# Expert loop of a hybrid layer: one-hot stationary gather with transposes, combining gates by transposes, gate and up biases on two row groups

## The reference, cut to what matters

```python
def swiglu_expert(xb, wg, bg, wu, bu, wd, bd):
    gate = jnp.minimum(xb @ wg + bg, SWIGLU_LIMIT)
    up = jnp.clip(xb @ wu + bu, -SWIGLU_LIMIT, SWIGLU_LIMIT)
    glu = gate * jax.nn.sigmoid(SWIGLU_ALPHA * gate)
    return ((up + 1.0) * glu) @ wd + bd

# routed_moe: logits = hf @ wr + br; top_v, top_i = lax.top_k(logits, 4)
# gates = jax.nn.softmax(top_v); the output of a token is the sum over its
# four experts of gate * swiglu_expert(token)
```

## Time and profile before

| | |
|---|---|
| time, median of three runs | 1285.4 us (1281.82 to 1287.41) |
| span of the profiled execution | 1284.3 us |
| TensorE busy | 1223.1 us, 95% of the span |
| VectorE, ScalarE, GpSimd busy | 250.6, 183.5, 19.8 us |
| L1431, weight products, 3072 records | 456.1 + 226.8 us |
| L1415, gather, 1056 records | 128.5 us |
| L1424, biases, 256 records | 69.6 us |
| L1406, spread, 66 records | 37.0 us |
| moved by DMA | 455.34 MB, 355 GB/s over the span |

### The profile page before, as it was taken

The page is one execution under the profiler, slowest core; times in us unless marked ns, Lnnn a source line. Parts: engine busy times, 40 slices in busy tenths (PEclk is TensorE's granted clock), DMA queues, the critical chain, the costliest instruction groups (busy, mean ns, idle before and its releaser), DMA issues.

```text
span 1284.3 us, 15147 instructions
## 1 busy us (share of the span) xinstructions
PE 1223.1 (95%) x6020; PEld 552.0 (43%) x6020; DVE 250.6 (20%) x535; ACT 183.5 (14%) x305; POOL 19.8 (2%) x40
## 2 busy tenths in 40 slices
PE   6699999999999999999999999999999999999995
PEld 1388965543333334443333333333333333333332
DVE  1334571511111111111111111111111111111113
ACT  1122431201111111111111111111111111111111
POOL 3000000000000000000000000000000000000000
PEclk9599999969999999999999999999999999999998
DMA  9994359529999999999999999999999999999971
GB/s 316 333 331 140 118 202 360 197 110 373 398 407 406 406 407 405 403 409 408 405 407 406 405 408 403 405 404 410 405 404 408 407 406 406 407 408 406 405 303 33
DMA packets 135160, 455.34 MB, mean 355 GB/s; under 512 B 7967, under 2 KB 21299, under 8 KB 135014
## 3 DMA queue, kind: packets, MB, share of 16 engines
q1 hardware_dynamic: 132080, 446.73, 89.3%
q0 software_dynamic: 2064, 6.98, 1.6%
q10 hardware_dynamic: 998, 1.37, 0.4%
HBM read 453.35 MB, written 1.70 MB: 354 GB/s over the span
## 4 chain that ended last, share of the span: by engine, by line
PE 82%; ACT 3%; DVE 1%; issue 0%
PE bank L1431 53%; PE bank L1415 10%; PE bank L1424 5%; PE bank L1441 5%; PE bank L1406 3%; PE bank L1307 2%; ACT k_pool L623 1%; PE bank L1102 1%; ACT at_pool L615 1%; PE bank L1134 1%; PE bank L1109 1%; PE bank L1463 0%; PE bank L1375 0%; PE bank L1343 0%; DVE xres L1063 0%; DVE k_pool L1062 0%
## 5 line engine op out<-in xcount | busy, mean ns | idle before, releaser
L1431 PE MATMUL bank<-ring,at_pool 128*64 128x512 f32 x2048 | 456.1, 598 | 0.0
L1431 PEld LDWEIGHTS bank<-ring,at_pool 128*64 128x64 f32 x2048 | 141.9, 137 | 310.5 <-issue 310.5
L1431 PE MATMUL bank<-ring,k_pool 128*64 128x512 f32 x1024 | 226.8, 595 | 23.0 <-ACT k_pool L623 23.0
L1431 PEld LDWEIGHTS bank<-ring,k_pool 128*64 128x64 f32 x1024 | 70.7, 137 | 158.5 <-issue 127.9
L1415 PEld LDWEIGHTS bank<-keyT,rows 128*128 128x128 f32 x1056 | 123.7, 196 | 28.6 <-issue 28.6
L1005 DVE TENSOR_SCALAR k_pool<-bank 128x512 f32<-128x512 f32 x32 | 22.1, 692 | 578.9 <-PE bank L1431 578.9
L1415 PE MATMUL bank<-keyT,rows 128*128 128x64 f32 x1056 | 128.5, 281 | 0.0
L615 ACT COPY at_pool<-bank 128x512 f32<-128x512 f32 x33 | 19.3, 586 | 443.3 <-PE bank L1415 443.3
L1424 PE MATMUL bank<-kv_pool,cumT 32*64 32x512 f32 x256 | 69.6, 620 | 0.0
L1009 DVE TENSOR_SCALAR k_pool<-bank 128x512 f32<-128x512 f32 x32 | 22.1, 692 | 226.9 <-PE bank L1431 226.9
L1441 PE MATMUL bank<-d_pool,at_pool 64*128 64x512 f32 x264 | 65.6, 615 | 0.7 <-ACT d_pool L625 0.7
(11 more groups left out here) (300 smaller groups left out, 590.5 us busy)
## 6 DMA issues: line engine op xcount, KB each, us to landing
ring<-in_w_gate SPq DMA_DIRECT2D x128, 1024.0 KB, 9.5
ring<-in_w_up SPq DMA_DIRECT2D x128, 1024.0 KB, 8.7
ring<-in_w_down SPq DMA_DIRECT2D x128, 1024.0 KB, 7.4
ring<-in_w_mod SPq DMA_DIRECT2D x24, 1024.0 KB, 10.1
ring<-in_w_in SPq DMA_DIRECT2D x13, 1024.0 KB, 12.5
ring<-in_w_out SPq DMA_DIRECT2D x4, 1024.0 KB, 6.7
k_pool<-in_const_masks POOLq DMA_DIRECT2D x1, 1024.0 KB, 8.0
g<-in_b_mod POOLq DMA_DIRECT2D x2, 512.0 KB, 12.3
```

The costliest lines, as they stand in the source:

```text
L1431: ins = mm(bank[CAP * half:CAP * (half + 1), :], lhsT(2 * r + kk), w[:, kk, 512 * half:512 * (half + 1)], start=m == 2 and r == 0 and kk = ...
```

## The change

- The gather takes the one-hot matrix `Ptok` (128x64) as the stationary operand and 512 columns of `rows` as the moving one: four matmuls into bank 3, which then holds the tokens in rows, its two halves of columns on the two halves of the partitions. ScalarE copies them to `xg`, four transposes bring them into bank 1 (`tokens_transpose`), ScalarE copies that to `xe`.
- The gates: VectorE makes `Gtok`, tokens x slots (twice over, 128 columns) with the gate in place of the one, and two transposes give its transpose in bank 0; `slot_gates` is one copy. `spread`, and the transposes and copy of the ranks ahead of the loop, are gone.
- The biases of gate and up lie on partitions 0 to 31 and 32 to 63, `pick` has 64 rows, and the four bias matmuls of both stand together ahead of the gate product (`biases`).
- The order on TensorE is now: biases, gate product, combine, up product, gather, gate transposes, transposes of the activations, token transposes, down product. VectorE does `up_step` ahead of `slot_gates`. ScalarE does sigmoid, copy to `xg`, copy to `aT`, copy to `xe`, copy to `ysb`.
- The identity of the expert numbers comes with the constants and no longer from GpSimd. One `keep_clock` matmul ahead of the loop is gone.

The core of the diff:

```diff
+        bias_gu = moe_pool[0:2 * NE, 0:D]
+        bias_d = moe_pool[0:NE, D:2 * D]
+        xg = moe_pool[:, 2 * D:2 * D + 512]
+        Gtok = moe_pool[:, 2 * D + 512:2 * D + 768].rearrange("p (t s) -> p t s", t=2)
...
             with act.Fori(0, NE) as e:
                 sigmoid_step(e)
+                gathered_out(e + 1)
+                activations_out(e)
                 tokens_out(e + 1)
-                down_steps(e)
+                down_out(e)
...
+                slots = cst[:, C_SLOTROW:C_SLOTROW + P]
                 for t in range(2):
...
+                    r = rank[:, t, bass.ds(e, 1)] if off is None else rank_off[:, t:t + 1]
+                    V.tensor_scalar(Ptok[:, t, :], slots[:, 0:CAP], r, None, ALU.is_equal)
+                    ins = V.tensor_scalar(Gtok[:, t, :], slots, r, gate[:, t, bass.ds(e, 1)], ALU.is_equal, ALU.mult)
                 ins.then_inc(ev("route_ready"), 1)
...
+            def slot_gates(count, buf, bank=B[0]):
+                dve.wait_ge(ev("gT_ps"), count + 1)
+                V.tensor_copy(gT[:, buf, :], bank[:, 256:512]).then_inc(ev("gT_ready"), 1)
...
                     gate_step(e)
-                    dve.wait_ge(ev("xe_ps"), e + 1)
+                    dve.wait_ge(ev("gT_ps"), e + 1)
                     route(e + 1, 1 - u)
+                    up_step(e)
                     slot_gates(e + 1, 1 - u)
-                    up_step(e)
...
+            def gather(count):
                 pe.wait_ge(ev("route_ready"), count + 1)
-                mm(B[3], pick[:, buf, :], rgT, start=True, stop=True).then_inc(ev("bc_ps"), 1)
+                pe.wait_ge(ev("xg_sb"), count)
+                for t in range(2):
+                    for half in range(2):
+                        ins = mm(B[3][CAP * half:CAP * (half + 1), :], Ptok[:, t, :], rows[:, t, 512 * half:512 * (half + 1)],
+                                 start=t == 0, stop=t == 1)
+                ins.then_inc(ev("xg_ps"), 1)
+            def gates_transpose(count, emptied, bank=B[0]):
+                pe.wait_ge(ev("gate_min"), emptied)
+                pe.wait_ge(ev("gT_ready"), count)
+                for t in range(2):
+                    ins = tr(bank[:, 256 + P * t:256 + P * (t + 1)], Gtok[:, t, :], ident)
+                ins.then_inc(ev("gT_ps"), 1)
+            def tokens_transpose(count):
+                pe.wait_ge(ev("xg_sb"), count + 1)
+                pe.wait_ge(ev("xe_ready"), count)
+                for q in range(4):
+                    ins = tr(B[1][:, P * q:P * (q + 1)], xg[:, P * q:P * (q + 1)], ident)
+                ins.then_inc(ev("xe_ps"), 1)
+            def biases(buf, count):
                 pe.wait_ge(ev("gT_ready"), count + 1)
+                pe.wait_ge(ev("xe_ready"), count + 1)
+                for m in range(2):
+                    r = slice(NE * m, NE * (m + 1))
+                    for half in range(2):
+                        mm(B[m][CAP * half:CAP * (half + 1), :], pick[r, buf, :], bias_gu[r, 512 * half:512 * (half + 1)],
+                           start=True, stop=False)
...
             open_sums(0)
-            gather(0, between=lambda: open_sums(1))
-            keep_clock(1, B[2])
+            pe.wait_ge(ev("gT_ready"), 1)
+            tokens_transpose(0)
+            open_sums(1)
...
                     e = i * 2 + u
-                    pe.wait_ge(ev("xe_ready"), e + 1)
-                    product(B[0], 0, u, xe_tile, e)
+                    biases(u, e)
+                    product(B[0], 0, xe_tile, e)
                     combine(1 - u, e + 1)
-                    spread(1 - u, e + 1)
-                    product(B[1], 1, u, xe_tile, e)
+                    product(B[1], 1, xe_tile, e)
                     gather(e + 1)
-                    down(u, e)
+                    gates_transpose(e + 1, e + 1)
+                    activations_transpose(e)
+                    tokens_transpose(e + 1)
+                    down(e)
```

More of the change, by code:

```diff
@@ L442, in _ @@
             pool.wait_ge(ev("cat_ps"), 4)
[L443 to L444 removed]
+            small_load("mbias_loaded", bias_gu[0:NE, :], b_gate[0])
+            small_load("mbias_loaded", bias_gu[NE:2 * NE, :], b_up[0])
+            small_load("mbias_loaded", bias_d, b_down[0])
             pool.wait_ge(ev("mbias_loaded"), 48)
@@ L609, in _, with gathered_out @@
             act.wait_ge(ev("rgT_ps"), 1)
-            nc.scalar.copy(rgT, B[1][0:NE, :]).then_inc(ev("rgT_ready"), 1)
+            nc.scalar.copy(gateT, B[1][0:NE, 0:2 * P]).then_inc(ev("gateT_ready"), 1)
+            def gathered_out(count):
+                act.wait_ge(ev("xg_ps"), count + 1)
+                nc.scalar.copy(xg, B[3]).then_inc(ev("xg_sb"), 1)
             def tokens_out(count):
                 act.wait_ge(ev("xe_ps"), count + 1)
-                nc.scalar.copy(xe.rearrange("p k s -> p (k s)"), B[3]).then_inc(ev("xe_ready"), 1)
+                nc.scalar.copy(xe.rearrange("p c s -> p (c s)"), B[1]).then_inc(ev("xe_ready"), 1)
             def sigmoid_step(count):
@@ L1394, in _ @@
             for t in range(2):
-                tr(B[1][0:NE, P * t:P * (t + 1)], rank[:, t, 0:NE], ident)
-                ins = tr(B[1][0:NE, 256 + P * t:256 + P * (t + 1)], gate[:, t, :], ident)
+                ins = tr(B[1][0:NE, P * t:P * (t + 1)], gate[:, t, 0:NE], ident)
             ins.then_inc(ev("rgT_ps"), 1)
             mm(B[0][:, 64:65], cst[:, C_STRI:C_STRI + P], flag, start=True, stop=True).then_inc(ev("pos_ps"), 1)
-            def spread(buf, count):
+            def gather(count):
@@ L1405, in spread @@
                 pe.wait_ge(ev("route_ready"), count + 1)
-                mm(B[3], pick[:, buf, :], rgT, start=True, stop=True).then_inc(ev("bc_ps"), 1)
-            def gather(count, between=None):
-                pe.wait_ge(ev("gT_ready"), count + 1)
[L1411 to L1424, removed]
+                pe.wait_ge(ev("xg_sb"), count)
[3 more added lines that the diff above has]
+                                 start=t == 0, stop=t == 1)
@@ new lines, in biases, with product @@
+            def biases(buf, count):
+                pe.wait_ge(ev("gT_ready"), count + 1)
+                pe.wait_ge(ev("xe_ready"), count + 1)
[4 more added lines that the diff above has]
+                           start=True, stop=False)
+            def product(bank, m, lhsT, count):
@@ L1444, in xe_tile, with activations_transpose @@
             def xe_tile(k):
-                return xe[:, k, :]
+                return xe[:, k % 4, CAP * (k // 4):CAP * (k // 4 + 1)]
             def a_tile(k):
                 return aT[:, k % 4, CAP * (k // 4):CAP * (k // 4 + 1)]
-            def down(buf, count):
+            def activations_transpose(count):
                 pe.wait_ge(ev("a_ready"), count + 1)
@@ L1455, in down @@
                 ins.then_inc(ev("aT_ps"), 1)
+            def down(count):
                 pe.wait_ge(ev("aT_ready"), count + 1)
-                product(B[2], 2, buf, a_tile, count)
+                product(B[2], 2, a_tile, count)
             def open_sums(t):
                 for half in range(2):
-                    mm(B[4 + 2 * t + half], rgT[:, 256 + P * t:256 + P * (t + 1)], mbias[:, 2, 512 * half:512 * (half + 1)],
+                    mm(B[4 + 2 * t + half], gateT[:, P * t:P * (t + 1)], bias_d[:, 512 * half:512 * (half + 1)],
                        start=True, stop=False)
             keep_clock(2, B[2])
-            pe.wait_ge(ev("rgT_ready"), 1)
-            spread(0, 0)
+            gather(0)
+            pe.wait_ge(ev("gateT_ready"), 1)
+            gates_transpose(0, 0, B[1])
             pe.wait_ge(ev("onehot_ready"), 1)
@@ L1495, in _ @@
                     with pe.If(n_over > j):
-                        spread(0, j + (NE + 1))
                         gather(j + (NE + 1))
[L1498 to L1501, removed]
+                        gates_transpose(j + (NE + 1), j + NE)
+                        tokens_transpose(j + (NE + 1))
+                        biases(0, j + (NE + 1))
+                        product(B[0], 0, xe_tile, j + NE)
+                        product(B[1], 1, xe_tile, j + NE)
+                        activations_transpose(j + NE)
+                        down(j + NE)
                         combine(0, j + (NE + 2))
```

69 lines of the change are left out of this document (30 added, 39 removed).

## The result

Over four runs each, the changed kernel takes 1245.6 us (1242.4 to 1249.6), the one before 1283.6 (1281.3 to 1287.4): a ratio of 0.970, interval 0.967 to 0.972. The profiled execution has a span of 1241.7 us and a time of 1243.5. The forecast was 1241 of time and 1239.8 of span.

The account below looks back on a forecast made before the run. TensorE set the pace (30.97 us per expert), loads close behind (30.6); after the change the loads set the end. First issue 270, loads 951.3, tail 1.8 and 16.7: span 1239.8, plus 1.1 makes 1241 us, range 1227 to 1256.

Parts of the forecast that it names:

- TensorE per expert, 27.7 us: Expert loop: TensorE's time per expert falls from 30.97 us by savings of 1.05 (spread), 1.0 (biases) and 1.2 (up-to-down stretch).
- The loads take over after about seven experts: Expert loop: load slack of some 20 us shrinks 2.9 us an expert; once gone, TensorE waits at 30.6 us per expert.
- First issue, 270: Start of the loop: the first ring slot is refilled at 270 us instead of 278.59, a gain of 8.6 us.
- Loads at 411 GB/s, 946.4 us: Expert loop: after the first load's 4.9 us, 371 more loads at 2.551 us each take 946.4 us.
- Rival 1: Expert loop: loads run at 406 GB/s, not 411, so 371 loads take 958.2 us and the time is 1253; 9%.
- Tail, a quarter of a product behind the last load: End of the loop: 1.8 us of product after the last load, then 16.7 us from the last result's copy.
- Rival 2: Expert loop: without overlap of biases and gather halves, TensorE still sets the end at 30.4 us per expert, time 1260; 6%.
- Rival 3: Expert loop: with 12 loads outstanding the queue gives 424 GB/s, 2.473 us a load, time 1212; 6%.
- Rival 4: Expert loop: TensorE's waits for loads drop its clock to 1.2 GHz; six such experts give 1359 us, slower; 5%.
- The 358 GB/s: Load rate: the skill page's HBM limit for a core, called contradicted by the trace's 406 GB/s over 800 us.
- The last 1.1 us, from span to time: Whole kernel: the median of the runs lies 1.1 us above the span, added to 1239.8 to give 1241.

Follow-up runs that it names:

- experiment 1: SP's loads of the second expert held back to a later point, in the changed kernel (1260.1 us, ratio 0.983) and in the kernel before (1286.0 us, ratio 1.002).
- experiment 4: The changed kernel with half of every w_down chunk of the experts not loaded, TensorE's program as it is: 1168.4 us, ratio 0.910 to the kernel before.
- experiment 5: The changed kernel with 8 KB pieces, down-bias opening sums moved into the loop, zero matmuls for four clock-keeping ones: 1213.8 us, ratio 0.944 to the kernel before.

## Why the prediction was right, step by step

- *TensorE per expert, 27.7 us:* 27.63. The biases overlap in full across 32-row groups (1.02 us for all four), the gather takes 1.8, down starts 3.74 us behind the up product (3.75 forecast), with the small wait for VectorE that was named (0.16). VectorE's longer route is hidden, as is the token copy.
- *The loads take over after about seven experts:* the first wait of any length is in the gate product at 457.96, the eighth.
- *First issue, 270:* 266.42; the forecast was 3.6 too late. The bounds held (266 to 273). 1.4 of the 3.6 is the luck of this execution: it ran ahead of that of the kernel before already in front of everything that the change touches, at the first transposes of the router's chain (before, then after):

```profile
239.78 1.05 PE L1368 MATMUL bank<-cst,rows 128*128 128x128 f32 x8
...
238.41 1.05 PE L1379 MATMUL bank<-cst,rows 128*128 128x128 f32 x8
```

  Over the ten profiled executions of all the kernels here these transposes start between 236.73 and 241.43. From there to the first bias sum the change costs 0.78, about the 0.95 forecast. For the other 2.2 I chose from the wrong end: the granted clock did fall again, at about 262 and not at 259.3, and was back at 265.5 instead of 279.5. Only the biases and the first product met it:

```profile
260.00:262.00 2.00, 2.00 (x8) 0.58 (x10) 0.00 (x0) 1.68 (x2) 0.00 (x0) 1.00 0.00 0
262.00:264.00 2.00, 2.00 (x10) 0.29 (x4) 0.00 (x0) 0.00 (x0) 0.00 (x0) 0.52 0.00 0
264.00:266.00 2.00, 2.00 (x8) 0.61 (x6) 0.00 (x0) 0.00 (x0) 0.00 (x0) 0.63 0.03 8
```

- *Loads at 411 GB/s, 946.4 us:* at the 410 of the page, 371 loads take 948.8, 2.4 more. Rival 1, 406 as the true rate, falls: the spells of the earlier trace rows were an empty queue, since they are gone, also in the kernel before once its loads are held back (410 in experiment 1).
- *Tail, a quarter of a product behind the last load:* mis-sized. The last load lands, by the sum 266.42 + 4.9 + 948.8, at 1220.1, and the rate does fall to 115 GB/s in 1220 to 1222. But the copy stands at 1225.06, 4.9 behind it and not 1.8. The last wait is for the up product's fourth chunk (1212.41); behind it come 1.8 us of product, 3.7 of gather and transposes and 7.1 of down product, in which the down chunks land unseen. That is 3.1 more.
- Together - 3.6 + 2.4 + 3.1 = + 1.9, which is the span's 1241.7 against 1239.8. So the mechanism was right and the single terms were each off by 2 to 4 us; that the sum came so close is luck, since the errors had opposite signs and 1.4 of the first was this execution's own.
- *Rival 2* falls with the overlap, and TensorE alone would end at 1166 (experiment 4). *Rival 3:* the fuller queue brought nothing (410 with a landing time of 18.3 us, 410 to 411 with 8.5). *Rival 4:* the granted clock is 1.00 in every window from 266 to 1222 us, with waits of 0.25 to 0.6 us at four chunks of every expert. The Trainium skill's warning ("TensorE: Matmul & The Clock Gate", Loop structure matters more than you think) does not reach waits as short as these, by this trace.
- *The 358 GB/s* that the prediction calls contradicted: one core ran here, alone. That it moves 410 shows that 358 does not bound such a core, and nothing about cores that load side by side.
- *The last 1.1 us, from span to time:* too small. The median of the runs is 3.9 us above the span of the profiled one: each of the four runs' times is 1.8 us above its own span (1243.5 against 1241.7 here), and the profiled execution was the second shortest of the four. The four spans are 1240.6 to 1247.8, the longer with the lower mean clock (0.985 at the shortest, 0.977 at the longest). That fits a first issue that moves with the clock ahead of the loop; only one of the four has a trace, so this is not shown.

## What to carry to other kernels

When two resources are both near full, compute the period of each from its own rows, and then the end from the one that takes over, with what is already loaded when the stage begins: here a ring full with one expert of 32 and an issue 12 us earlier turned 3.3 us saved per expert into 42, not into 105 and not into 11 (32 x 0.35). Once the transfers set the end, their first issue, their bytes and their rate decide it, with what must still follow the last wait (here 12.6 us, from 1212.41 to the copy at 1225.06); holding the transfers back for a moment is a cheap test of that, and it says more than a busy share. The larger pieces were worth nothing, and even a loss, until TensorE's part was made.

## What the runs showed of the hardware that I had not expected

- Pieces of 8 KB moved 422 GB/s where pieces of 4 KB moved 410, both with the queue never empty: 2.9% more. The profile counts 135160 packets with the one and 86008 with the other, 49152 fewer, which is half of the 98304 pieces of 4 KB: each piece is one packet. A fixed time per piece fits: the 349 GB/s of 1 KB pieces early in the trace and the 410 of 4 KB give, as an estimate, the 422 of the expectation. The Trainium skill, "DMA: Bandwidth & Descriptors", Why small descriptors are slow, gives some three cycles of overhead per packet and 32 bytes of descriptor per DMA operation. Between 4 KB (131 cycles with the three) and 8 KB (259) that would be an estimated 1.2%, or 1.5% with the descriptors: the trace has about twice that.
- Reading every second column costs TensorE little but not nothing: four transposes 0.75 us instead of 0.66, and 0.2 us over a gather of 16 stationary operands.
- With zero matmuls in place of four clock-keeping ones and the opening sums moved away, the granted clock stayed at 1.00 from 256 to 268 in experiment 5, the only such execution with a trace. In the changed kernel, with the opening sums and the biases ahead of it, it fell at about 262. Why it falls there is open.
